# The up projection's bias moved from TensorE products into a row copied to 96 partitions and added by VectorE

## The reference

```
def expert_block(args):
    xblk, e = args
    hu = xblk @ w_up_gate[e] + b_up_gate[e]          # 1024 -> 2048
    g, u = hu[:, :D_FF_EXPERT], hu[:, D_FF_EXPERT:]
    g = jnp.minimum(g, SWIGLU_LIMIT)
    u = jnp.clip(u, -SWIGLU_LIMIT, SWIGLU_LIMIT)
    act = g * jax.nn.sigmoid(SWIGLU_ALPHA * g) * (u + 1.0)
    return act @ w_down[e] + b_down[e]
```

## Time and profile before

| what | value |
|---|---|
| median of 3 runs | 1817.23 us (1815.08 to 1819.37) |
| profiled execution, its own time | 1818.09 us |
| its span | 1816.3 us |
| busy in the span | PE 1766.9, DVE 1435.2, ACT 1145.6, POOL 307.7 us |
| bytes by DMA | 488.44 MB |

### The profile page before, as it was taken

One profiled execution on the slowest core, in us unless ns is written; L12 is line 12 of the kernel. 1 busy time (PEld: TensorE's weight loads), 2 busy tenths in 40 slices (PEclk: granted clock), 3 DMA queues, 4 the chain that ended last, 5 costly groups with the idle time before them and its releaser, 6 DMA issues.

```text
span 1816.3 us, 26680 instructions
## 1 busy us (share of the span) xinstructions
PE 1766.9 (97%) x9009; PEld 1297.3 (71%) x9009; DVE 1435.2 (79%) x1492; ACT 1145.6 (63%) x1118; POOL 307.7 (17%) x240
## 2 busy tenths in 40 slices
PE   6999999999999889999999999999999999999995
PEld 5777777777778757777777777777777777777764
DVE  4565676576657688988888898889888988888888
ACT  4534554464454457777777777777777777777772
POOL 0012102210210111111211121112111111211150
PEclk9999999999999899999999999999999999999997
DMA  7431333133125479999999999999999999999995
GB/s 204 128 98 42 104 95 90 56 105 92 47 94 205 147 265 353 391 370 372 361 355 374 374 364 353 373 362 360 367 373 365 362 364 364 378 348 374 367 343 217
DMA packets 158914, 488.44 MB, mean 269 GB/s; under 512 B 13170, under 2 KB 83106, under 8 KB 125376
## 3 DMA queue, kind: packets, MB, share of 16 engines
q1 hardware_dynamic: 151792, 471.48, 71.4%
q0 software_dynamic: 7088, 16.52, 2.7%
HBM read 479.43 MB, written 24.39 MB: 277 GB/s over the span
## 4 chain that ended last, share of the span: by engine, by line
PE 92%; DVE 4%; DMA 2%; ACT 1%; issue 1%; SPq 0%; POOL 0%; DVEq 0%; POOLq 0%; ACTq 0%
PE psum L304 27%; PE psum L306 26%; PE psum L305 26%; PE psum L930 2%; PE psum L664 1%; PE psum L694 1%; PE psum L680 1%; PE psum L954 1%; PE psum L914 1%; DVE hres L1873 1%; PE psum L647 1%; PE psum L631 1%; PE psum L966 1%; DMA x2d<-xr 1%; PE psum L641 1%
## 5 line engine op out<-in xcount | busy, mean ns | idle before, releaser
L1612 DVE TENSOR_TENSOR wL<-wraw,wH 128x2048 fp32r<-128x2048 f32 x388 | 883.9, 2290 | 129.6 <-ACT wH L403 129.4
L403 ACT ACTIVATE wH<-wraw 128x2048 fp32r<-128x2048 f32 x388 | 743.9, 1919 | 308.8 <-PE psum L306 300.9
L304 PE MATMUL psum<-wH,xTH 128*96 128x512 f32 x1040 | 417.3, 401 | 1.4 <-DVE wL L1612 1.3
L306 PE MATMUL psum<-wH,xTL 128*96 128x512 f32 x1040 | 409.0, 393 | 0.0
L305 PE MATMUL psum<-wL,xTH 128*96 128x512 f32 x1040 | 408.9, 393 | 0.0
L304 PEld LDWEIGHTS psum<-wH,xTH 128*96 128x96 f32 x1040 | 168.4, 162 | 73.5 <-issue 2.2
L306 PEld LDWEIGHTS psum<-wH,xTL 128*96 128x96 f32 x1040 | 168.2, 162 | 72.6
L305 PEld LDWEIGHTS psum<-wL,xTH 128*96 128x96 f32 x1040 | 168.4, 162 | 69.7
L304 PE MATMUL psum<-wH,aTH 128*96 128x512 f32 x496 | 201.3, 406 | 0.0
L306 PE MATMUL psum<-wH,aTL 128*96 128x512 f32 x496 | 194.6, 392 | 0.0
L305 PE MATMUL psum<-wL,aTH 128*96 128x512 f32 x496 | 194.2, 391 | 0.0
(11 more groups left out here) (257 smaller groups left out, 2201.6 us busy)
## 6 DMA issues: line engine op xcount, KB each, us to landing
wraw<-in_w_up_gate SPq DMA_DIRECT2D x256, 1024.0 KB, 7.0
wraw<-in_w_down SPq DMA_DIRECT2D x128, 1024.0 KB, 7.5
fraw<-in_w_in SPq DMA_DIRECT2D x68, 512.0 KB, 4.1
yd<-in_consts SPq DMA_DIRECT2D x8, 1024.0 KB, 8.0
wraw<-yd SPq DMA_DIRECT2D x4, 2048.0 KB, 8.2
wraw<-in_w_out SPq DMA_DIRECT2D x4, 1024.0 KB, 6.0
xt<-in_x SPq DMA_DIRECT2D x4, 512.0 KB, 5.9
hres<-in_x SPq DMA_DIRECT2D x4, 512.0 KB, 6.9
```

Source lines behind the costliest of these rows:

```text
L304: nc.tensor.matmul(ps, lh, rh, start=start, stop=False)
L306: return nc.tensor.matmul(ps, ll, rh, start=False, stop=stop)
L403: nc.scalar.activation(wH[:, b % SPLIT, :], raw(b), ACT.Copy).then_inc(p_hi, 1)
L1612: V.tensor_tensor(wL[:, b % SPLIT, :], raw(b), wH[:, b % SPLIT, :].bitcast(F32), ALU.subtract).then_inc(p_lo, 1)
```

## The change

`b_up_gate` no longer goes through the three-part split. For each expert SyncE copies its row of 2048 float32 to 96 partitions (`bub`, 0.79 MB), VectorE adds its first half to the gate half of the PSUM result into `sg`, and its second half and 1 to the other half into `ucl`, and clips `ucl` in place; `silu` now works in place on `sg`. TensorE's wait for the banks becomes one for `ub_ready`. The split that is left has 1024 columns in place of 3072. `bub` lies where `hot_slot` was, hence SyncE's wait for `tabT_done`.

```diff
-BIAS_STEPS = 6
+BIAS_STEPS = 5
@@ SyncE
             for r in range(3):
-                sp.dma_start(braw[r * NE:(r + 1) * NE, 0:2 * FF], b_up_gate[0]).then_inc(b_in, 16)
-                sp.dma_start(braw[r * NE:(r + 1) * NE, 2 * FF:], b_down[0]).then_inc(b_in, 16)
+                sp.dma_start(braw[r * NE:(r + 1) * NE, :], b_down[0]).then_inc(b_in, 16)
...
+            def load_up_bias(i, e):
+                sp.wait_ge(tabT_done, 1)
+                if not first(i):
+                    sp.wait_ge(ub_ready, i)
+                sp.dma_start(bub[0:BLK, :], b_up_gate[0][bass.ds(e, 1), :].to_broadcast([BLK, 2 * FF])).then_inc(bub_in, 16)
             def load_body(e):
                 for p in range(8):
                     load_piece(e, p, up_src(e, p))
+                    if p == 0:
+                        load_up_bias(e - 1, e - 1)
@@ TensorE, up_part
                 if not first(i):
-                    pe.wait_ge(ucl_ready, i)
-                    pe.wait_ge(sg_ready, i)
-                pe.wait_ge(sel_ready[0], i + 1)
+                    pe.wait_ge(ub_ready, i)
...
-                for n in range(4):
-                    nc.tensor.matmul(bank[n][0:BLK, :], sel[:, 0, 0:BLK], bias[:, n * 512:(n + 1) * 512], start=True, stop=False)
...
-                        last = mm3(bank[n][0:BLK, :], xTH[:, p, :], xTL[:, p, :], wH[:, slot, cols], wL[:, slot, cols], False, p == 7)
+                        last = mm3(bank[n][0:BLK, :], xTH[:, p, :], xTL[:, p, :], wH[:, slot, cols], wL[:, slot, cols], p == 0, p == 7)
@@ ScalarE
             def silu(i, over=False):
-                act.wait_ge(p_used, used(up_at(i, over), 8))
-                if not first(i):
-                    act.wait_ge(act_ready, i)
-                A(sg[0:BLK, :], hu[0:BLK, 0:FF], ACT.Silu, scale=ALPHA).then_inc(sg_ready, 1)
+                act.wait_ge(gb_ready, i + 1)
+                A(sg[0:BLK, :], sg[0:BLK, :], ACT.Silu, scale=ALPHA).then_inc(sg_ready, 1)
@@ VectorE
-            V.tensor_scalar(braw[:, FF:2 * FF], braw[:, FF:2 * FF], 1.0, None, ALU.add).then_inc(b_step, 1)
...
             def clip_up(i, over=False):
...
-                V.tensor_scalar(ucl[0:BLK, :], hu[0:BLK, FF:2 * FF], 1.0 + LIMIT, 1.0 - LIMIT, ALU.min, ALU.max).then_inc(ucl_ready, 1)
+                dve.wait_ge(bub_in, 16 * i + 16)
+                V.tensor_tensor(sg[0:BLK, :], hu[0:BLK, 0:FF], bub[0:BLK, 0:FF], ALU.add).then_inc(gb_ready, 1)
+                V.scalar_tensor_tensor(out=ucl[0:BLK, :], in0=hu[0:BLK, FF:2 * FF], scalar=1.0, in1=bub[0:BLK, FF:], op0=ALU.add,
+                                       op1=ALU.add).then_inc(ub_ready, 1)
+                dve.wait_ge(ub_ready, i + 1)
+                V.tensor_scalar(ucl[0:BLK, :], ucl[0:BLK, :], 1.0 + LIMIT, 1.0 - LIMIT, ALU.min, ALU.max).then_inc(ucl_ready, 1)
...
                 clip_up(i)
-                if prefetch:
-                    select(0, i + 1, None)
                 low_piece(i, 11)
```

More of the change, by code:

```diff
@@ L194, in build @@
     hres = sb("hres", [P, NT, D])
-    bias = sb("bias", [3 * NE, 3 * D], BF16)
+    bias = sb("bias", [3 * NE, D], BF16)
+    place = sb("place", [P, 2, T], F32R)
     tab = sb("tab", [P, NE * NBC, 2], I32)
-    sel = sb("sel", [3 * NE, 2, P], BF16)
+    sel = sb("sel", [3 * NE, P], BF16)
     ixg = sb("ixg", [P, 2], I32)
@@ L265, in build @@
     at[0] = small_top + 4 * 2 * FF * 4
-    braw = sb("braw", [3 * NE, 3 * D])
+    braw = sb("braw", [3 * NE, D])
     assert at[0] <= small_top + RAW * 2 * FF * 4
     at[0] = att_work
-    place = sb("place", [P, 2, T], F32R)
+    bub = sb("bub", [P, 2 * FF])
+    assert at[0] <= att_work + NT * TOPK * P * 4
+    at[0] = ngain_at
     yH0 = sb("yH0", [P, D], F32R)
-    assert at[0] <= att_work + NT * TOPK * P * 4
     at[0] = mid_top
@@ L347, in build @@
     p_hi, p_lo, p_used = sem("p_hi"), sem("p_lo"), sem("p_used")
-    sel_ready = sems("sel_ready", 2)
+    sel_ready, bub_in, gb_ready, ub_ready = sem("sel_ready"), sem("bub_in"), sem("gb_ready"), sem("ub_ready")
     ix_ready, xg_in, xg_zero = sem("ix_ready"), sem("xg_in"), sem("xg_zero")
@@ L547, in _ @@
                 load_piece(NE, q, down_src(NE - 1, q))
+                if q == 0:
+                    load_up_bias(NE - 1, NE - 1)
             sp.wait_ge(y_out, 16 * LATE[0])
@@ L561, in overflow @@
                     load_piece(i, 4 + p, up_src(e, p))
+                    if p == 0:
+                        load_up_bias(i, e)
                 for q in range(4):
@@ L960, in down_part @@
                 if isinstance(i, int) and i == LATE[1]:
-                    pe.wait_ge(sg_ready, NE)
+                    pe.wait_ge(ub_ready, NE)
                 elif not first(i) and not over:
                     pe.wait_ge(y_ready, i)
-                pe.wait_ge(sel_ready[1], i + 1)
+                pe.wait_ge(sel_ready, i + 1)
                 for n in range(2):
-                    nc.tensor.matmul(bank[yb + n][0:BLK, :], sel[:, 1, 0:BLK], bias[:, (4 + n) * 512:(5 + n) * 512], start=True, stop=False)
+                    nc.tensor.matmul(bank[yb + n][0:BLK, :], sel[:, 0:BLK], bias[:, n * 512:(n + 1) * 512], start=True, stop=False)
                 pe.wait_ge(aTl_ready, 2 * i + 2)
@@ L1213, in bias_high @@
                 if n == 0:
-                    act.wait_ge(b_in, 16 * 6)
-                act.wait_ge(b_step, 2 * n + 1)
+                    act.wait_ge(b_in, 16 * 3)
+                else:
+                    act.wait_ge(b_step, 2 * n)
                 A(bias[0:left, :], braw[0:left, :], ACT.Copy).then_inc(b_step, 1)
@@ L1636, in _ @@
             merged_low(7)
[L1637 to L1638 removed]
+            dve.wait_ge(b_in, 16 * 3)
             for n in range(2):
                 left = (2 - n) * NE
[L1641 removed]
+                dve.wait_ge(b_step, 2 * n + 1)
                 V.tensor_tensor(braw[0:left, :], braw[0:left, :], bias[0:left, :], ALU.subtract).then_inc(b_step, 1)
@@ L1662, in row_scale @@
             def row_scale(j):
-                dve.wait_ge(sd1, j + 1)
+                dve.wait_ge(sd1, 2 * j + 2)
                 V.reciprocal(stat[:, 28 + j:29 + j], stat[:, 24 + j:25 + j]).then_inc(rs1, 1)
@@ L1703, in first_low, with select @@
                                            op1=ALU.subtract).then_inc(xTl_ready, 1)
-            def select(s_, e, after):
+            def select(e, after):
                 if after is not None:
                     dve.wait_ge(p_used, after)
-                V.tensor_scalar(sel[:, s_, :], cst[0:3 * NE, bass.ds(K_SE + e, 1)].to_broadcast([3 * NE, P]), 1.0, None,
-                                ALU.mult).then_inc(sel_ready[s_], 1)
+                V.tensor_scalar(sel[:, :], cst[0:3 * NE, bass.ds(K_SE + e, 1)].to_broadcast([3 * NE, P]), 1.0, None,
+                                ALU.mult).then_inc(sel_ready, 1)
             add_rows(0)
@@ L1717, in _ @@
             scaled_rows(1)
-            select(0, 0, None)
             add_rows(2)
@@ L1826, in _ @@
             x_low(1)
-            select(0, 1, None)
-            select(1, 0, None)
+            select(0, None)
             swiglu(0)
@@ L1850, in body @@
                     low_piece(i + 1, 2)
-                select(1, i, BODY * i + 9)
+                select(i, BODY * i + 9)
             with dve.Fori(1, NE - 1) as i:
@@ L2077, in overflow @@
                 code = gp.snap(code)
+                gp.wait_ge(comb_done, NT * (i - (NE - 1)))
                 gather(i, code)
```

9 lines of the change are left out of this document (4 added, 5 removed).

## The result

The changed kernel took 1880.97 us (median of 4 runs, 1859.71 to 1886.57), the kernel before 1817.62 us (4 runs, 1815.08 to 1819.37): a ratio of 1.033, 95% interval [1.025, 1.041]. It is slower by 63 us where I had forecast 22 us less. The profiled execution took 1886.57 us with a span of 1884.7; it is the slowest of the four.

What follows compares the result with a forecast made beforehand. TensorE was taken to lead, with DMA nearly level. Split -8.4, gather +2.0, expert 1's wait +6.0, 29 bodies at -0.80 and end +1.8 sum to -21.8 us: 1818.1 becomes 1796, range 1782 to 1811.

Steps and rivals of the forecast that it cites:

- What bounds the kernel: Experts' stage: TensorE leads, other engines a little quicker; dropping four products takes 0.87 us off each body, to 35.00 us.
- VectorE: Each body: adds and clip take 1.7 us more, covered by slack; uncovered only after the last up projection, +1.8 us.
- The split: Ahead of the experts: bias split ends near 571.5 instead of 582.1, removing TensorE's wait and lower clock: -8.4 us.
- The first two bias loads: Experts 0 and 1: slower token gather for expert 1, +2.0 us, and VectorE standing 6 us for expert 1's row, +6.0 us.
- my two terms: Start of the experts: +2.0 us for the slower gather and +6.0 us for the wait at expert 1's bias row.
- The added loads: Steady bodies: 0.79 MB more needs 399 GB/s, taken as available; bodies of 35.07 us, saving 0.80 each.
- At that rate a body's bytes take 34.4 us: Steady bodies: at 406 GB/s, seen over 60 us, loads take 0.6 us less than TensorE's 35.00.
- some 1.9 us later: Steady bodies: bias row lands 1.9 us after the piece ahead, about 1223.6, 2.2 us before VectorE wants it.
- Rival 3: Steady bodies: 367 GB/s is all there is beside these loads; 38.0 us per body, 1877 in all; 8%, milder form included.

Runs made afterwards that it cites:

- neither: The changed kernel with the first matrix's bias left out entirely (no products, loads or adds), the split still shorter: 1783.5 us, ratio 0.981.
- once: The changed kernel with the bias row loaded for expert 0 only, all experts adding that row: 1787.6 us, ratio 0.983.

## Why the prediction was wrong

**What bounds the kernel: right.** TensorE led. With no load in the way, bodies fell to 34.94 and 34.97 us, with TensorE busy in all of them; I had said 35.00.

**VectorE: right in the bodies, too small at the end.** The prices were 1.22, 1.21 and 0.69 us, and bodies with the adds and no loads are as long as without (34.97 and 34.94). But the whole run costs 4 us over the run with neither, and the forecast had 1.8: the later `swiglu` alone. Behind the last `swiglu` a low part also waits for ScalarE's high part, 1.88 us with the adds and 0.28 without (first once, then neither):

```profile
1745.62 2.29 DVE L1617 TENSOR_TENSOR wL<-wraw,wH 128x2048 fp32r<-128x2048 f32 x1 [1.88 <-ACT wH L405]
```

```profile
1740.03 2.29 DVE L1618 TENSOR_TENSOR wL<-wraw,wH 128x2048 fp32r<-128x2048 f32 x1 [0.28 <-ACT wH L405]
```

In the changed kernel this makes most of the 2.1 us behind the last `swiglu`; the forecast had no term for it.

**The split: right.** I said -8.4 us. The run with neither reaches expert 0's `swiglu` 9.3 us earlier than the kernel before (650.5 and 659.8), 0.9 of it for the four products. The changed kernel has the adds in front of that `swiglu` and gained 7.5. A split made 4 us shorter, with nothing else changed, gave 7.6.

**The first two bias loads: right in kind, too small.** Expert 0's gather took 9.3 us instead of 9.07, so +0.3 and not +2.0. From expert 0's `swiglu` to expert 1's pass 41.6 us, and 34.0 in the run with expert 0's load alone: 7.6 us where I had 6.0. By expert 2's, the changed kernel has lost 12.6 us against the kernel before where my two terms made 8.0. VectorE stood before expert 1's row 8.3 us instead of 6:

```profile
688.68 1.22 DVE L1820 TENSOR_TENSOR sg<-psum,bub 96x1024 f32<-96x1024 f32 x1 [8.29 <-DMA bub<-in_b_up_gate]
```

**The added loads: the step that failed.** "At that rate a body's bytes take 34.4 us" took the 406 GB/s of the earlier trace rows as a property of the engines, to be had for any bytes. The rate depends on what is in the stream. With no bias load, or up to 0.39 MB of it in 96 partitions, the kernel asks for 373 to 383 GB/s and gets them (TensorE is busy 199 to 200 of 200 us). It needs 399 with the row, and gets 347 to 375 with 0.79 MB in 96 partitions, and 400 to 402 of the 406 that 1.05 MB in 128 need. From this one step come the 27 x 2.09 = 56 us, and the landing: "some 1.9 us later" than the piece ahead was 1254.25 - 1250.80 = 3.45 us, and that piece itself took 10.8 us instead of 6.7. So the row wasn't 2.2 us early but 4 to 5 us late.

**Rival 3** gave 1877 by 38.0 us per body, close to what happened; since its reason does not hold, that closeness is luck. Its sentence on the missing evidence (the 60 us of the earlier trace rows held no such load) did name the weak point. The reason, that 367 GB/s is all there is beside one row read 96 times, is refuted twice: by the different rows (no change) and by 128 partitions (400 GB/s with the same row read 128 times). I gave it 8%, because I weighed a rate from another mix above the rate of the stretch that I was forecasting. The 358 GB/s of the Trainium skill's HBM Reference (Specifications) that I had set aside would not have been the reason either: this core had 400 over 200 us.

**What stays open.** That rows of 8 KB to 96 partitions are dear and to 128 are not is shown, at two places in the queue and with and without adds. With 128 partitions the load is also as large as a weight piece, and no run kept the bytes and changed the partitions alone (128 rows of 6 KB, say), nor tried 64 partitions. Why 96 are dear is only argued. The Trainium skill offers a reading: SBUF — State Buffer (section "Door 1: The DMA port swizzle") says that partitions reach SBUF by 16 ports, with partition and partition + 32 on one port and + 64 on another, and DMA: Bandwidth & Descriptors (section "The descriptor swizzle") says that in a transfer to 128 partitions each engine writes one port of its own. By that map, as my estimate, 96 partitions load one half of the ports twice as much as the other, and 0.79 MB would take as long as 1.05 MB do. By this alone the changed kernel would be as fast as the run with 128 partitions; it was 71 us slower, so engines that meet at one port would have to slow each other. The packets that take twice their usual time are what this would look like, but the traces don't tell at what they meet. Nor is it known why the loads cost more where nobody waits for them (40.06 us per body) than where VectorE does (37.95). I suppose that the wait thins the queue out, but no run changed the queue's depth alone.

## What to carry to other kernels

Before a load is added to a full stream, ask how many partitions it goes to, not only how many bytes it has; loading rows that nobody uses can be the cheaper form, as it was here by 71 us. A GB/s figure from another stretch is evidence for that stretch's mix alone, and a DMA share of 1.0 does not say at what rate the engines are busy. And when an engine stands at a load, first try the case in which nobody waits for it: here that was slower, so the wait was not the cause.

## What the runs showed of the hardware that I had not expected

Loads of 96 rows of 8 KB took the stream from 373 down to 348 GB/s, though the kernel asked for more; with loads of 128 such rows it carried 400. One row read 96 times costs no more than 96 different rows (1926.9 and 1930.5 us). In short windows the stream reached 430 GB/s; DMA: Bandwidth & Descriptors of the Trainium skill (Rules for kernel authors) advises 128 partitions and 1 MiB or more per DMA for the highest bandwidth, and the trace agrees, with 400 GB/s against 362. GpSimd's copy of 128 x 2 numbers, 1.2 us before, took 8.15 us on average; VectorE had no gap while it ran. With adds and no loads it took 6.7 us, and bodies were no longer than without.
